# Turning the feed-forward inner tiles by VectorE squares and SBUF-to-SBUF transfers instead of TensorE transposes

## The reference, cut to what matters

```python
def swiglu(x, w_gate, w_up, w_down):
    return (jax.nn.silu(x @ w_gate) * (x @ w_up)) @ w_down

f = swiglu(rmsnorm(h, g_ffn1_pre[i]), w_ffn1_gate[i], w_ffn1_up[i], w_ffn1_down[i])
h = h + 0.5 * rmsnorm(f, g_ffn1_post[i])
... # attention
f = swiglu(rmsnorm(h, g_ffn2_pre[i]), w_ffn2_gate[i], w_ffn2_up[i], w_ffn2_down[i])
```

## Time and profile before

| | |
|---|---|
| median of 3 runs | 1909.64 us (1909.54 to 1910.44) |
| the profiled execution | 1910.02 us; its span 1908.2 us |
| granted TensorE clock | 0.999 of full speed |
| TensorE, VectorE, ScalarE busy | 99%, 55%, 46% of the span |
| HBM read | 358.01 MB, 189 GB/s over the span |

### The profile page before, as it was taken

The page is one execution under the profiler, slowest core; times in us unless marked ns, Lnnn a source line. Parts: engine busy times, 40 slices in busy tenths (PEclk is TensorE's granted clock), DMA queues, the critical chain, the costliest instruction groups (busy, mean ns, idle before and its releaser), DMA issues.

```text
span 1908.2 us, 24808 instructions
## 1 busy us (share of the span) xinstructions
PE 1896.6 (99%) x8818; PEld 1566.9 (82%) x8818; DVE 1058.5 (55%) x1188; ACT 885.4 (46%) x1199; POOL 112.6 (6%) x162
## 2 busy tenths in 40 slices
PE   9999999999999999999999999999999999999998
PEld 7888888888888888888888888888888888888886
DVE  5455445455444446777896744445544544444565
ACT  6444444444443445555565644444444444344563
POOL 1000000000000001012551100000000000000010
PEclk9999999999999999999999999999999999999999
DMA  7666666666656655655556566666666665656554
GB/s 255 188 189 192 189 188 186 187 189 191 196 196 201 198 194 165 199 173 165 154 176 206 165 199 189 188 189 189 189 191 187 187 194 195 204 195 203 195 188 144
DMA packets 188516, 361.05 MB, mean 189 GB/s; under 512 B 11472, under 2 KB 16032, under 8 KB 188064
## 3 DMA queue, kind: packets, MB, share of 16 engines
q1 hardware_dynamic: 187440, 356.69, 60.7%
q10 hardware_dynamic: 1008, 3.46, 0.5%
HBM read 358.01 MB, written 2.10 MB: 189 GB/s over the span
## 4 chain that ended last, share of the span: by engine, by line
PE 98%; DVE 1%; DMA 0%; SPq 0%; ACT 0%; issue 0%; DVEq 0%; POOLq 0%; POOL 0%; ACTq 0%
PE bank L516 31%; PE bank L518 31%; PE bank L517 31%; PE bank L620 1%; PE bank L829 1%; PE bank L858 1%; PE bank L840 1%; DMA resid<-in_x 0%; PE bank L804 0%; DVE w_rest L1317 0%; DVE x_rest L1332 0%; PE bank L579 0%; PE bank L589 0%; PE bank L593 0%; DVE resid L1341 0%; PE bank L554 0%
## 5 line engine op out<-in xcount | busy, mean ns | idle before, releaser
L1317 DVE TENSOR_TENSOR w_rest<-raw,w_high 128x1024 fp32r<-128x1024 f32 x654 | 802.7, 1229 | 741.7 <-ACT w_high L971 740.6
L971 ACT CAST w_high<-raw 128x1024 fp32r<-128x1024 f32 x654 | 684.6, 1049 | 881.4 <-PE bank L518 880.3
L516 PE MATMUL bank<-w_high,x_high 128*128 128x512 f32 (+1 forms) x1912 | 748.0, 391 | 0.7 <-DVE x_rest L1654 0.2
L518 PE MATMUL bank<-w_high,x_rest 128*128 128x512 f32 (+1 forms) x1912 | 741.7, 388 | 0.0
L517 PE MATMUL bank<-w_rest,x_high 128*128 128x512 f32 (+1 forms) x1912 | 740.9, 387 | 0.0
L518 PEld LDWEIGHTS bank<-w_high,x_rest 128*128 128x128 f32 x1912 | 359.0, 188 | 74.3
L516 PEld LDWEIGHTS bank<-w_high,x_high 128*128 128x128 f32 x1912 | 359.2, 188 | 73.7 <-issue 1.7
L517 PEld LDWEIGHTS bank<-w_rest,x_high 128*128 128x128 f32 x1912 | 359.4, 188 | 71.1
L516 PE MATMUL bank<-w_high,h_high 128*128 128x512 f32 x704 | 274.4, 390 | 0.0
L518 PE MATMUL bank<-w_high,h_rest 128*128 128x512 f32 x704 | 274.0, 389 | 0.0
L517 PE MATMUL bank<-w_rest,h_high 128*128 128x512 f32 x704 | 274.0, 389 | 0.0
(11 more groups left out here) (161 smaller groups left out, 747.6 us busy)
## 6 DMA issues: line engine op xcount, KB each, us to landing
raw<-in_w_ffn_up SPq DMA_DIRECT2D x176, 512.0 KB, 3.7
raw<-in_w_ffn_down SPq DMA_DIRECT2D x176, 512.0 KB, 4.4
raw<-in_w_ffn_gate SPq DMA_DIRECT2D x174, 512.0 KB, 4.4
raw<-in_w_qkv SPq DMA_DIRECT2D x68, 512.0 KB, 4.0
raw<-in_w_o SPq DMA_DIRECT2D x32, 512.0 KB, 4.3
raw<-in_w_ple_gate SPq DMA_DIRECT2D x32, 512.0 KB, 4.3
resid<-in_x SPq DMA_DIRECT2D x8, 256.0 KB, 7.6
gain_row<-in_g_ffn_post SPq DMA_DIRECT2D x8, 256.0 KB, 4.4
```

What stands on the lines that cost most here:

```text
L516: nc.tensor.matmul(o[:, 0:width], xh, wh, start=first and c == 0, stop=False)
L518: ins = nc.tensor.matmul(o[:, 0:width], xr, wh, start=False, stop=last and c == chunks - 1)
L971: nc.scalar.copy(slot(n, k)[0], raw[:, k]).then_inc(w_high_done, 1)
L1317: nc.vector.tensor_tensor(to_rest, raw[:, k], to_high.bitcast(F32), ALU.subtract).then_inc(w_rest_done, 1)
```

## The change

For the blocks 0 to 9 of each layer, TensorE no longer turns `hidden`. At the head of turn i of the loop, VectorE turns each 32x32 square of the block's two tiles in place of the squares' order (`squares_of`, two instructions of 128x512), into `squares_out`. A turned 128x128 tile also needs its squares exchanged between groups of 32 partitions: ScalarE issues 16 transfers from SBUF to SBUF (`move_hidden`), one for each pair of a target and a source group, each of 32 partitions with two runs of 512 B, behind the first two casts of the turn. They go into `moved`. Behind `silu` and four casts more, ScalarE waits for all 16 transfers and copies `moved` to `h_high` in one instruction of 128x1024 (`high_moved`), and VectorE subtracts in one (`rest_moved`). In ScalarE's turn of the loop the order is thus: casts of the slots n+4 and n+5, the 16 issues, casts of n+6 to n+10, silu, casts of n+11 to n+14, the copy, casts of n+15 to n+19. The down matmul waits for `moved_rest` for the chunks of blocks 0 to 9. The last block is turned by TensorE as before. Left out of the diff are the three places that only pass the layer's number `f` to ScalarE's `ffn`.

```diff
--- before.py
+++ after.py
@@ -96,10 +96,13 @@
     XU = KC // CPS
     U_X1 = 0
     U_H1 = U_X1 + XU
-    U_MIX = U_H1 + BPB * FB
+    U_MIX = U_H1 + BPB
     U_X2 = U_MIX + XU
     U_H2 = U_X2 + XU
-    U_P = U_H2 + BPB * FB
+    U_P = U_H2 + BPB
+    MOVED = FB - 1
+    SQ = 32
+    G = P // SQ
     U_PLE = U_P + 1
     S_TURN_P = 12
     UW = NB // BPB
@@ -205,6 +208,8 @@
         branch = sb("branch", [P, T, D])
         silu_g = branch[:, 0, 0:T * NB].rearrange("p (t n) -> p t n", t=T)
         hidden = branch[:, 1, 0:T * NB].rearrange("p (t n) -> p t n", t=T)
+        squares_out = branch[:, 0, T * NB:2 * T * NB].rearrange("p (t n) -> p t n", t=T)
+        moved = branch[:, 1, T * NB:2 * T * NB].rearrange("p (t g n) -> p t g n", t=T, g=G)
         gain_row = sb("gain_row", [P, 2, NB])
         ident = sb("ident", [P, P])
         G_FFN1, G_MIX, G_O, G_FFN2, G_PLE = (KC * k for k in range(NG))
@@ -306,6 +311,8 @@
         lead_resid, lead_turned = sem("lead_resid"), sem("lead_turned")
         lead_high, lead_rest = sem("lead_high"), sem("lead_rest")
         silu_ready, hidden_ready = sem("silu_ready"), sem("hidden_ready")
+        squares_ready, moved_landed = sem("squares_ready"), sem("moved_landed")
+        moved_high, moved_rest = sem("moved_high"), sem("moved_rest")
         squared, rstd_ready = sem("squared"), sem("rstd_ready")
         half_out, branch_ready = sem("half_out"), sem("branch_ready")
         z_ready, swap_ready = sem("z_ready"), sem("swap_ready")
@@ -718,10 +725,10 @@
                 n = (NG - 1) * KC
                 nc.tensor.transpose(turn[3][:, 0:n], gain_in, ident[0:n, 0:n]).then_inc(gain_turned, 1)
 
-            def turn_hidden(i, u_h, f):
-
-                pe.wait_ge(hidden_ready, f * FB + i)
-                pe.wait_ge(turn_rest, u_h - BPB + BPB * i)
+            def turn_hidden(u_h, f):
+
+                pe.wait_ge(hidden_ready, f * FB + FB)
+                pe.wait_ge(turn_rest, u_h)
                 for j in range(BPB):
                     turn_chunks(lambda t, c: hidden[:, t, (CPS * j + c) * P:(CPS * j + c + 1) * P], turn[j])
 
@@ -745,8 +752,6 @@
                     pe.wait_ge(silu_ready, f * FB + i)
                     for s in range(KS):
                         use_slot(n + s, s % RING, x_high, x_rest, CPS * s, even, s == 0, s == KS - 1)
-                        if s == 1:
-                            turn_hidden(i, u_h, f)
                     pe.wait_ge(hidden_ready, f * FB + i)
                     for s in range(KS):
                         use_slot(n + KS + s, s % RING, x_high, x_rest, CPS * s, odd, s == 0, s == KS - 1)
@@ -759,12 +764,14 @@
 
                     pe.wait_ge(branch_ready, CREDIT - 1 + 2 * NBD * f + nb)
                     for s in range(FS - last if nb == NBD - 1 else FS):
-                        if nb == 0:
-                            pe.wait_ge(turn_rest, u_h + s + 1)
+                        if nb == 0 and s < BPB * MOVED:
+                            pe.wait_ge(moved_rest, f * MOVED + s // BPB + 1)
+                        elif nb == 0:
+                            pe.wait_ge(turn_rest, u_h + s - BPB * MOVED + 1)
                         use_slot(n + s, (k0 + s) % RING, h_high, h_rest, CPS * s, acc[(b0 + nb) % 2],
                                  s == 0, s == FS - 1)
                         if nb == 0 and s == 0:
-                            turn_hidden(FB, u_h, f)
+                            turn_hidden(u_h, f)
                         if f and nb == NBD - 1 and s == S_TURN_P:
                             turn_p()
                 use_last_slots(n + FS - last, (k0 + FS - last) % RING, h_high, h_rest, CPS * (FS - last),
@@ -1045,12 +1052,27 @@
                                                    scale=rstd[:, job, t:t + 1])
                     ins.then_inc(silu_ready, 1)
 
-                def hidden_high(i):
+                def last_high():
 
                     for j in range(BPB):
-                        act.wait_ge(turned, u_h - BPB + j + 1 + BPB * i)
-                        nc.scalar.copy(h_high[:, bass.ds(CB * i - CB + CPS * j, CPS), :],
+                        act.wait_ge(turned, u_h + j + 1)
+                        nc.scalar.copy(h_high[:, CB * MOVED + CPS * j:CB * MOVED + CPS * (j + 1), :],
                                        turn[j][:].rearrange("p (c s) -> p c s", c=CPS)).then_inc(turn_high, 1)
+
+                def move_hidden(i):
+
+                    act.wait_ge(squares_ready, f * MOVED + i)
+                    for g in range(G):
+                        for r in range(G):
+                            nc.scalar.dma_start(moved[g * SQ:(g + 1) * SQ, :, r, :],
+                                         squares_out[r * SQ:(r + 1) * SQ, :, g * P:(g + 1) * P]
+                                         ).then_inc(moved_landed, 16)
+
+                def high_moved(i):
+
+                    act.wait_ge(moved_landed, 16 * G * G * (f * MOVED + i))
+                    nc.scalar.copy(h_high[:, bass.ds(CB * i - CB, CB), :].rearrange("p c (r b) -> p c r b", b=SQ),
+                                   moved.rearrange("p t g (c b) -> p c (t g) b", c=CB)).then_inc(moved_high, 1)
 
 
                 ahead(n0, KS - RING, RING - 1)
@@ -1062,12 +1084,14 @@
                         between(m)
                 with act.Fori(1, FB) as i:
                     n = n0 + 2 * KS * i
-                    ahead(n, 0, 3)
-                    hidden_high(i)
-                    ahead(n, 3, KS - 4)
+                    ahead(n, 0, 2)
+                    move_hidden(i)
+                    ahead(n, 2, KS - 3)
                     silu(i)
-                    ahead(n, KS - 1, KS + 1)
-                hidden_high(FB)
+                    ahead(n, KS - 1, 4)
+                    high_moved(i)
+                    ahead(n, KS + 3, KS - 3)
+                last_high()
 
             def down(n0, b0, job, f):
                 for nb in range(NBD):
@@ -1430,11 +1454,28 @@
                                                              op0=ALU.mult, op1=ALU.mult)
                     ins.then_inc(hidden_ready, 1)
 
-                def hidden_rest(i):
+                def squares_of(i):
+
+                    dve.wait_ge(hidden_ready, f * FB + i)
+                    for t in range(T):
+                        ins = nc.vector.transpose(squares_out[:, t, :].rearrange("p (g c b) -> p g c b", g=G, c=CB),
+                                                  hidden[:, t, :].rearrange("p (c g b) -> p g c b", g=G, c=CB))
+                    ins.then_inc(squares_ready, 1)
+
+                def rest_moved(i):
+
+                    chunks = bass.ds(CB * i - CB, CB)
+                    dve.wait_ge(moved_high, f * MOVED + i)
+                    nc.vector.tensor_tensor(h_rest[:, chunks, :].rearrange("p c (r b) -> p c r b", b=SQ),
+                                            moved.rearrange("p t g (c b) -> p c (t g) b", c=CB),
+                                            h_high[:, chunks, :].bitcast(F32).rearrange("p c (r b) -> p c r b", b=SQ),
+                                            ALU.subtract).then_inc(moved_rest, 1)
+
+                def last_rest():
 
                     for j in range(BPB):
-                        chunks = bass.ds(CB * i - CB + CPS * j, CPS)
-                        dve.wait_ge(turn_high, u_h - BPB + j + 1 + BPB * i)
+                        chunks = slice(CB * MOVED + CPS * j, CB * MOVED + CPS * (j + 1))
+                        dve.wait_ge(turn_high, u_h + j + 1)
                         nc.vector.tensor_tensor(h_rest[:, chunks, :], turn[j][:].rearrange("p (c s) -> p c s", c=CPS),
                                                 h_high[:, chunks, :].bitcast(F32), ALU.subtract).then_inc(turn_rest, 1)
 
@@ -1448,12 +1489,13 @@
                 ahead(n0, 2 * KS - 1, 1)
                 with dve.Fori(1, FB) as i:
                     n = n0 + 2 * KS * i
-                    ahead(n, 0, 3)
-                    hidden_rest(i)
-                    ahead(n, 3, 2 * KS - 4)
+                    squares_of(i)
+                    ahead(n, 0, KS + 3)
+                    rest_moved(i)
+                    ahead(n, KS + 3, KS - 4)
                     gate_up(i)
                     ahead(n, 2 * KS - 1, 1)
-                hidden_rest(FB)
+                last_rest()
 
             def down(n0, b0, job, f):
 
```

More of the change, by code:

```diff
@@ L1038, in boundary, with ffn @@
                         high(n0 + RING + k - LEAD + 2, k - LEAD + 2)
-            def ffn(n0, b0, u_h, job, between=None):
+            def ffn(n0, b0, u_h, job, f, between=None):
                 def silu(i):
@@ L1155, in load_small @@
                                   ).then_inc(sinks_landed, 16)
-            ffn(S_FFN1, 0, U_H1, J_IN1, load_small)
+            ffn(S_FFN1, 0, U_H1, J_IN1, 0, load_small)
             down(S_DOWN1, 2 * FB, J_POST1, 0)
@@ L1247, in _ @@
             boundary(U_X2, G_FFN2, S_FFN2, J_IN2, 1, square_mix)
-            ffn(S_FFN2, B_FFN2, U_H2, J_IN2)
```

(1 more changed line is left out.)

## The result

Slower: 1965.79 us (4 runs, 1964.12 to 1966.83) against 1909.84 before, ratio 1.0292, 95% interval 1.0274 to 1.031. That is 56 us more where 18.6 less were forecast, and outside the stated range. The profiled execution after took 1966.62 us with a span of 1964.8.

What follows compares the result with a forecast made beforehand. TensorE was taken to bound the kernel; removed transposes save 18.6 us and everything added hides in idle time, so 1910.02 - 18.6 = 1891.4 us profiled, 1891.0 us measured. Stated range: 1889.5 to 1914 us.

Steps and rivals of the forecast that it cites:

- The bound: TensorE has work for 99% of the span and the chain runs on it for 98%, so only it sets the time.
- the gain: Removing 8 TensorE transposes a turn, 10 turns in two layers, saves 20 x 0.93 = 18.6 us.
- the term that was called decisive: 16 transfers issued in a row on ScalarE's queue before the cast of slot n+6; free up to 0.51 us each.
- The window: On ScalarE's queue, from 5.66 us until the cast must start by 13.91 us, the issues have 8.18 us.
- The price: One issue on ScalarE's queue taken as 0.38 us, 6.1 us for 16; bounds 0.33 and 0.74 us.
- Rival A: The issues fill the DMA queues and hold ScalarE up: about 1920 us, or 1965 us if all are slow; chance 0.17.
- B: Smaller hold-up on ScalarE's queue, 0.52 to 0.56 us an issue: 1893 to 1907 us; chance 0.04 of faster.
- its harder case: All 16 issues on ScalarE's queue cost 0.74 us: 3.7 - 0.93 = 2.7 us a block, 1965 us.
- Its deciding price, 0.57 us: Issue price on ScalarE's queue at which the gain is gone: (8.18 + 0.93)/16 = 0.57 us.
- C: Transfers land one after another, delaying ScalarE's copy; decides at 2.0 us each, some 1920 to 2320 us; chance 0.02.
- D: VectorE's square transposes are late: over 2.4 us each for a stall, gain gone above 2.9; chance 0.03.
- E: TensorE's path isn't shortened because something else, such as weights, lies just behind; excluded within 1%, no separate chance given.

Runs made afterwards that it cites:

- the three late trains: Changed kernel with 14 or 15 of its 16 transfers kept in a row, and with all 16: 1913.99, 1926.61 and 1965.79 us.
- The four wide transfers: Changed kernel with 4 transfers of 128 partitions, two runs of 512 B, without exchange between groups, in place of the 16: 1892.12 us.
- the spread ones: Changed kernel with the 16 issues handed out among ScalarE's casts, two or four at a time, not in a row: 1891.59 and 1891.42 us.
- the kernel with one run: Changed kernel with each of the 16 transfers having one run of 1 KB per partition instead of two of 512 B: 1961.46 us.

## Why the prediction was wrong

**The bound, the gain, the place: right.** TensorE set the time, the transposes were worth 18.2 us (18.6 forecast), and the term that was called decisive was.

**The window: right.** 8.18 us for the train was worked out from the timeline; 7.73 fits, 9.01 makes TensorE 0.9 us late, and the three late trains put it at 8.12. The pause follows from it: 16 x 0.647 - 8.18 = 2.17 us, 2.19 measured. Two small terms of it, 0.07 us for the wait and 0.10 for the handover, stood in none of the rows; in the timelines above the cast comes 0.20 us after the train's end (116.30 to 116.50) and TensorE starts 0.05 us after the rest is made (118.81 to 118.86), 0.08 more than the two.

**The price: wrong, and this is the step that failed.** "I take 0.38 us, a usual ScalarE issue with a gap of 0.05": it was 0.65. Every row that the price came from, on either queue, had one end in HBM; no transfer of the trace before had both in SBUF. A train adds to the price as well: from HBM the first issue took 0.32 us and the later ones 0.45, so that even there the step was 0.47, close to SP's 0.49 in the earlier trace rows. That row was named and set aside for a single issue's. Of the 0.27 us that were missing, about 0.09 are thus the train and 0.17 the two ends in SBUF. (The two don't simply add up: with both ends in SBUF the first issue of the train already took 0.60 us.) The train alone would not have upset the forecast: at 0.47 us, 16 issues fit, and the kernels with one end in HBM ran in 1891.6 and 1891.1 us. It is the two ends in SBUF that carried the price over 0.51. The prediction's upper bound, 0.74 us, held the measured price, but rivals A and B together had only 0.21 of the chances.

**Rival A: the right place, near the right time, the wrong mechanism.** It stood at 0.17 and its harder case at 1965 us. But no queue filled: the DMA engines were 0.56 busy, and within the block shown all 16 issues took 0.60 to 0.62 us, the last as the second. Its deciding price, 0.57 us, was nearly right: an estimate from the trains is 8.12 us of window and 0.93 of gain less 0.1 for the slower first matmul, some 8.9 us or 0.56 an issue. That the time came out like the 0.74 us case is luck; it did only because of what follows.

**A term left out.** The pause's price was taken as its length. Over the 20 blocks the matmul behind the train came 45.2 us late in all, 2.2 us a block in the first layer and 2.3 in the second, which brings 1891.5 to 1936.7. Of the 29 to 30 us from there to 1966, 27.7 are TensorE's slower matmuls behind the pause: 0.1 us a block for the slower start that followed every pause, and 24.9 more in the 17 blocks where the clock fell (in the block shown the two together are 1.7 us). About 2 us I have not placed. The kernel with 15 issues, whose pause is 0.6 us shorter, has no fall in any block. But the length of the pause alone doesn't decide it, since three pauses of the same length were not followed by one; what else does was not tried.

**Rivals C, D, E: fell as argued.** The transfers landed 1.9 to 3.9 us after their issue, overlapping; the squares took 0.69 us each (0.7 taken); without transfers the time falls by the whole gain. No other cover failed: the weight loads, the copy at 1.05 us and the subtraction at 1.23 stayed hidden. The Trainium skill's rule of gathering small transfers ("DMA: Bandwidth & Descriptors", section "Rules for kernel authors") pointed the right way. The four wide transfers show that it is the count of issues on a queue that had to fit, not the bytes: 4 of 128 KB took 2.70 us in all.

**The versions that beat both kernels** are the spread ones and those on SP's queue, all within 1891.0 to 1891.6 us: 0.95 to 0.98% faster than before, with the full computation.

## What to carry to other kernels

Count the issues of transfers as instructions in the order of the engine that issues them, and hold their sum against how late the next thing behind them may be; take the price of one from a train and with both ends where they will be. A train that overruns its slack by 2 us can be free when it is handed out between the waits that the engine has anyway, or put on the queue whose next item has more slack. And price a pause of TensorE by its length and by the matmuls behind it, over all blocks and not in one alone.

## What the runs showed of the hardware

- In a train, an issue with both ends in SBUF took 0.60 to 0.62 us on ScalarE's queue and a median of 0.60 on SP's; with one end in HBM, 0.32 for the first of a train and 0.45 for most of the next ones.
- ScalarE's queue issues transfers while the cast in front of them runs: 2.54 us of issues and 1.05 us of cast in a slot of 2.72 us, none late.
- After 2.03 us of idle time TensorE's granted clock fell from 2.4 to 1.2 GHz for eight matmuls (0.43 us apart) in the block shown. With 16 issues (2.02 to 2.18 us idle) it fell in 17 of 20 blocks, in the kernel with one run (1.85 to 1.96) in 16 of 20; with 15 issues (1.38 to 1.53) it stayed at 2.4 in all 20.
- VectorE turns 32x32 squares of float32, 128x512, in 0.69 us, the time of a two-input operation of that size.
